# All 37 steps of the sample selection placed in the prompt attention, none in the first sample attention

## What is computed

```python
kx_past = pool_idx[page_table, layer].reshape(n, past, IDX_DIM)
_, idx = lax.top_k(indexer_scores(qx, concatenate([kx_past, kx], axis=1), wx, q_pos), ksel)
...
return gathered_softmax(q, kg, vg, q_pos[None, :, None] - idx, bias_tab)
```

## Time and profile before

| what | us |
|---|---|
| median of 3 runs (lowest, highest) | 3109.66 (3102.31, 3110.35) |
| the profiled execution's own time | 3110.44 |
| its span, first to last instruction | 3108.7 |
| PE busy, share of the span | 2667.9 (86%) |
| DVE busy, share of the span | 1139.3 (37%) |
| ACT busy, share of the span | 667.5 (21%) |
| POOL busy, share of the span | 373.4 (12%) |

### The profile page before, as it was taken

One profiled execution on the slowest core, in us unless ns is written; L12 is line 12 of the kernel. 1 busy time (PEld: TensorE's weight loads), 2 busy tenths in 40 slices (PEclk: granted clock), 3 DMA queues, 4 the chain that ended last, 5 costly groups with the idle time before them and its releaser, 6 DMA issues. The chain is left out here.

```text
span 3108.7 us, 34294 instructions
## 1 busy us (share of the span) xinstructions
PE 2667.9 (86%) x13764; PEld 1720.2 (55%) x13764; DVE 1139.3 (37%) x2070; ACT 667.5 (21%) x1356; POOL 373.4 (12%) x362
## 2 busy tenths in 40 slices
PE   6989989284788897886648669999999999999998
PEld 4444444142577776454325334566666666888843
DVE  0677889512466764584615113100000000000133
ACT  3222220032344543674303200100000000000011
POOL 1000000102434431000026510000000000000000
PEclk9999999686799998898769879999999999999999
DMA  6100101331345443405769762310110112110010
GB/s 249 47 35 35 43 30 43 127 84 58 95 125 159 127 127 105 135 29 169 252 203 377 287 231 102 115 41 27 40 40 27 40 40 95 38 38 30 11 34 33
DMA packets 169652, 304.83 MB, mean 98 GB/s; under 512 B 48536, under 2 KB 120408, under 8 KB 167226
## 3 DMA queue, kind: packets, MB, share of 16 engines
q1 hardware_dynamic: 143714, 172.54, 17.7%
q0 software_dynamic: 23936, 95.29, 8.4%
q10 hardware_dynamic: 1864, 35.08, 3.3%
HBM read 262.23 MB, written 67.77 MB: 106 GB/s over the span
## 5 line engine op out<-in xcount | busy, mean ns | idle before, releaser
L1020 PE MATMUL m_B<-m_big,m_wdB 128*128 128x363 f32 (+1 forms) x2112 | 646.1, 468 | 3.2 <-issue 3.2
L1020 PEld LDWEIGHTS m_B<-m_big,m_wdB 128*128 128x128 f32 x2112 | 400.5, 190 | 247.9 <-issue 4.8
L458 PE MATMUL i_psM<-i_w,i_xnT 128*128 128x462 f32 (+2 forms) x1152 | 424.7, 527 | 2.6 <-ACT i_xnT L288 2.3
L458 PEld LDWEIGHTS i_psM<-i_w,i_xnT 128*128 128x128 f32 x1152 | 219.0, 193 | 199.0 <-issue 179.0
L882 DVE TENSOR_TENSOR m_actT<-m_wdB,m_B 128x363 f32 (+3 forms) x66 | 35.2, 533 | 604.1 <-PE m_B L1020 604.1
L421 DVE MAX8 i_top<-i_work 128x8 f32<-128x384 f32 (+5 forms) x186 | 166.4, 894 | 6.3
L422 DVE MATCH_REPLACE8 i_work<-i_top,i_work 128x384 f32<-128x384 f32 (+5 forms) x186 | 162.8, 875 | 0.0
L774 ACT ACTIVATE m_wdB<-m_B 128x363 f32<-128x363 f32 (+1 forms) x66 | 31.2, 473 | 598.9 <-PE m_B L1020 598.9
L1062 PE MATMUL m_B<-m_wdA,m_actT 128*128 128x256 f32 x704 | 152.4, 379 | 0.8 <-DVE m_actT L882 0.8
L1062 PE MATMUL m_B<-m_wdB,m_actT 128*128 128x256 f32 x704 | 152.6, 379 | 0.0
L740 POOL TENSOR_TENSOR m_rstd<-m_ms,m_half 128x1 f32<-128x1 f32 x18 | 9.9, 551 | 1133.0 <-DVE m_ms L850 1133.0
(11 more groups left out here) (413 smaller groups left out, 3532.5 us busy)
## 6 DMA issues: line engine op xcount, KB each, us to landing
b_Kp<-b_k SPq DMA_DIRECT2D x32, 512.0 KB, 11.4
b_Vp<-b_v SPq DMA_DIRECT2D x32, 512.0 KB, 10.9
o_bk<-b_k ACTq DMA_DIRECT2D x8, 2040.0 KB
o_bv<-b_v ACTq DMA_DIRECT2D x8, 2040.0 KB
m_wdB<-w_gate SPq DMA_DIRECT2D x22, 512.0 KB, 3.9
m_wdB<-w_up SPq DMA_DIRECT2D x22, 512.0 KB, 5.2
i_w<-w_in POOLq DMA_DIRECT2D x5, 1848.0 KB, 35.5
proj<-i_stage SPq DMA_DIRECT2D x40, 231.0 KB, 2.0
```

What stands on the lines that cost most here:

```text
L458: mm = nc.tensor.matmul(psM[:, q % 2, 0:cols.stop - cols.start], xnT[:, t % RING, k, :], w[:, k, cols], start=(k == 0), stop=(k == KO - 1))
L1020: mm = nc.tensor.matmul(B[:, bank, 0:r1 - r0], wgu[:, i, u, k, :], hnT[:, k, r0:r1], start=(k == 0), stop=(k == KO - 1))
```

## The change

`S_EARLY` becomes `S_STEPS`: all 37 steps are spread over the 32 pairs of the prompt attention by the same weights. The first sample attention does no steps; its DVE begins with the memset that releases POOL's stores of the mask. Nothing else is changed, and no operation is added or dropped.

```diff
-S_EARLY = 22
+S_EARLY = S_STEPS
...
                     dve.wait_ge(S["own"], own_n[0])
 
-                steps = iter(range(S_EARLY, S_STEPS))
-
-                def select(count):
-                    for _, k in zip(range(count), steps):
-                        kth.step(own, k)
-                        if k == S_STEPS - 1:
-                            nc.vector.memset(kth.count[:, :], 0.0).then_inc(s_steps, 1)
-
                 def evac_keys(k, i):
...
                     nc.vector.tensor_copy(spreadb[:, :, :], spread[:, :, :]).then_inc(spread_at, 1)
+                else:
+                    nc.vector.memset(kth.count[:, :], 0.0).then_inc(s_steps, 1)
                 dve.wait_ge(turned, 1)
...
-                    if not sparse:
-                        select(2)
```

## The result

The changed kernel takes 3123.66 us (median of 5 runs, 3122.43 to 3129.28), the kernel before 3106.38 (5 runs, 3100.86 to 3110.35): the ratio over the runs is 1.0060, interval 1.0043 to 1.0077. By the medians it is slower by 17.3 us; the forecast was slower by 18.6, which made 3129 us on top of a profiled execution of 3110.4. The profiled execution took 3123.41 us, span 3121.6, 13.0 us more than the one of before.

The account below looks back on a forecast made before the run. No engine alone bounds the prompt: DVE fills pairs with steps, PE sets the others; DVE delays only the sample stage's end. 28.5 - 1.0 - 8.9 = +18.6 us on 3110.4 gave 3129, range 3117 to 3143.

Parts of the forecast that it names:

- Pairs 0 to 30: Prompt loop turns before the final one: added steps cost +28.5 us, 16.0 of 44.5 us fitting into DVE's waits.
- busy time divided by 0.947: Prompt stretches with steps in nearly every pair: DVE fills them, so they last its busy time divided by 0.947.
- Tail: Behind the prompt's final logits: -1.0 us, at most 1.7, as PE and ACT arrive with less backlog.
- the cover that I named: Prompt's tail: 1.7 us of PE and ACT work hides the longer steps ahead of the last reciprocal.
- Sample stage: First sample attention: without its steps the last softmax starts 8.9 us earlier, ends 6.8 and 10.5.
- "nothing" for the stores: Sample stage's front: POOL's mask stores among the first key loads cost nothing, up to +3.9 us without cover.
- the fixed chain: Sample stage behind the last softmax: value products and loads of values hang on it and move along unchanged.
- Step 0's wait: Prompt: step 0 moves from pair 5 to pair 3 with its wait for the scores, which costs nothing.
- Rival 1: Prompt: steps fill every DVE wait, costing only +18.1 us; total 3119, or 3117 with further ends; chance 0.13.
- Rival 2: Prompt tiles 5 to 7: PE idles and its clock falls to 1.2 GHz, priced at +10 us, 3139; chance 0.18.
- the fall at 1421.8: Kernel before, prompt's end: clock drops to 1.2 GHz after PE was busy 1.40 of 3.50 us, taken as support.
- Rival 3: Sample stage: its 15 steps held up all of it, so removal gives back 49.6 us, 3088; chance 0.04.

Follow-up runs that it names:

- e6: Against the kernel before: 17 steps in pairs 0 to 30, at most one each, 4 in the final pair, 16 at the sample stage's front; 3096.25 us, ratio 0.9958.
- e10: e6 with the release of the mask's stores moved behind the logits of chunk 5; 3092.44 us, ratio 0.9945 to the kernel before.
- e9: Against the kernel before: no steps in pairs 0 to 30, 4 in the final pair, 33 in the first sample attention; 3133.21 us, pairs 0 to 30 146.28.
- e3: The changed kernel with the memset that releases the mask's stores moved behind the last chunk's logits; 3127.94 us in one run, sample stage 132.03.
- e8: The changed kernel with the memset that releases the mask's stores moved behind the logits of chunk 5; 3122.04 us, ratio 1.0041 to the kernel before.
- e7: The changed kernel with its 37 steps spread evenly, one in every pair, two in pairs 9, 20 and 30, three in the final; 3126.56 us, pairs 0 to 30 173.83.
- e2: The kernel before without the 15 steps of its first sample attention, the mask set to zeros instead; 3099.08 us, ratio 0.9972, sample stage 130.71.

## Why the prediction was right

**Pairs 0 to 30: right, 1.7 us too high.** Forecast +28.5, measured +26.76. For tile 4 the changed kernel took 24.95 against a forecast of 24.8, for tile 5 29.07 against 29.3, tile 6 33.51 against 33.6, tile 7 26.08 against 26.2. The rule "busy time divided by 0.947" is what these tiles show (27.55 / 29.07 = 0.948; 31.77 / 33.51 = 0.948; tiles 4 and 7 show 0.935 and 0.954). The overshoot is in the early tiles: +1.2 instead of +2.0 in tiles 0-1 and 36.82 instead of 37.5 us in tiles 2-3. PE may work off more of its lag there than I allowed; no run shows it. Of 44.5 us added, 17.7 found room; I had said 16.0.

**Tail: right in sign, the reason half wrong.** Forecast -1.0 by less backlog, at most 1.7; measured -1.67. By the rows the final pair's first value products start 0.88 us sooner after the logits (1444.13 - 1436.95 = 7.18, before 1421.65 - 1413.59 = 8.06): that fits the smaller backlog that I named. They take 1.97 us instead of 3.62, as the clock is high here (mean 1.00 from 1436.95 to 1454.25) and was low before (0.90 over its final pair): -1.65, which I had not counted, although show the fall in front of them. Against that the reciprocal comes late by 1.39 - 0.53 = 0.86: the cover that I named was used up by that much. -0.88 - 1.65 + 0.86 = -1.67. e6 and e10 (low clock, tail 19.5) and e9 (high, 17.9), all three with four bit steps in the final pair and an early reciprocal, agree with that part. So the size of the tail is partly luck. Why the clock falls there in some kernels only is open: PE's last two gaps ahead of these products are 1.11 and 1.29 us in the kernel before and in the changed one alike.

**Sample stage: the size right (-8.9 against -8.8), two of its steps wrong.** The removed steps gave what was said: from the end of the products to the softmax 1.60 us instead of 10.48, -8.88. But "nothing" for the stores failed, and so did the fixed chain in which the value products were to move along. The stores stood among the first loads of keys, ACT's first move came at 22.35 us after the stage's start instead of 21.69, and the keys ended 2.75 us later (87.63 against 84.88); ACT's own issues were no cover, as the later loads of keys were waited for as well (17.5 us against 14.8). And from the softmax to the next stage it took 42.25 us instead of 44.91, -2.66. e3 and e8 show that these belong together: the kernel before pays for the stores too, among its values, and e8, which has them out of the way, takes 42.38 us (1588.03 - 1545.65). -8.88 + 2.75 - 2.66 = -8.79. The size came out right by luck: two errors made up for each other.

The Trainium skill, page "DMA: Bandwidth & Descriptors", section "Rules for kernel authors", says that spreading DMAs over the issuing engines gains no bandwidth, as all run on the same 16 DMA engines and interleave. The runs agree: POOL's 0.53 MB of stores lengthened the stage among SP's loads at either place, and the gap was worth 4.1 and 4.6 us in e8 (against the changed kernel and e3) and 3.3 in e10 (against e6).

**Step 0's wait:** its cost of nothing stands; DVE waits for nothing but products and its own `k_cut` (0.4 us) in these pairs.

**Rival 1** (floor +18.1) would have needed every wait of DVE. 13.8 us of them are still there, and e7 shows that even an even spread doesn't reach the floor. Its further end is 3116.3 us (3110.4 + 18.1 - 1.7 - 10.5), not 3117, which changes nothing.

**Rival 2** (the clock) happened in part, and cost nothing that the rows show. In pairs 0 to 30 the granted clock fell to its low level, 1.2 GHz, six times for a short while, once in each stretch from tiles 2-3 to tile 6 and twice in tile 7; ahead of each fall PE had waited 1.8 to 3.6 us for DVE (2.92 in tile 6). PE's waits for DVE in the prompt, before and after (us, times, longest):

```profile
PE p_psS L2509 <- DVE p_mx L2472: 5.6, 7, 1.5
```

```profile
PE p_psS L2509 <- DVE p_mx L2472: 22.6, 14, 3.6
```

By the means of 0.92, 0.95 and 0.87 the clock was low for a tenth to a quarter of tiles 5 to 7, where the rival's price took half. Busy time by stretch of tile 6's four pairs in the changed kernel (pairs 24, 25 and 27 have two steps, pair 26 one):

```profile
1377.36:1386.61 9.25, 7.99 (x82) 5.84 (x80) 8.76 (x21) 6.20 (x15) 0.00 (x0) 1.00 0.05 18
1386.61:1395.80 9.19, 6.46 (x33) 3.28 (x35) 8.70 (x21) 4.34 (x12) 0.00 (x0) 0.81 0.03 9
1395.80:1401.68 5.88, 5.55 (x48) 3.33 (x45) 5.60 (x15) 3.31 (x8) 0.00 (x0) 1.00 0.22 56
1401.68:1410.87 9.19, 8.31 (x89) 6.01 (x86) 8.70 (x21) 6.38 (x16) 0.00 (x0) 1.00 0.04 14
```

Pair 25, with a mean clock of 0.81, is as long as pair 27 at 1.00, and pair 24 as long as the 9.25 us of the earlier trace rows. DVE fills all three, and pair 25's products for keys still came after PE had waited 2.92 us for DVE. That is the room that the prediction set against this rival, though in tiles 5 to 7 it is about a quarter (24.55 busy in 33.6 leaves 27%) and not a third. The Trainium skill, page "TensorE: Matmul & The Clock Gate", section "Why this matters for your kernels", warns against idle gaps of PE between bursts of matmuls, since they halve the clock. The six falls agree in so far as each came behind such a gap. The fall at 1421.8, which the prediction set beside it, is a weaker case, as the same gaps of 1.11 and 1.29 us brought no fall in the changed kernel. The time of rival 2 did not follow, since another engine was the bound.

**Rival 3** is out by e2: all steps together hold the stage up by 9.6 us, not by 49.6.

## What to carry to other kernels

Work that is moved into another engine's shadow is free only up to the time that this engine needs, pair by pair: the first 17 steps cost 0.4 us in all, the last 12 bit steps with two finish steps 26.8. So before moving, compare what room the target has in each turn with what the old place really pays (9.6 of an estimated 49.6 us here), and split the work by that. A store that nobody waits for belongs where the DMA engines idle, not at the front of a stage or at its end.

## What was not expected of the hardware

- Six falls of the granted clock (means by tile of 0.87 to 0.95) left no trace where DVE fills the pairs: pair 25 took 9.19 us at 0.81 and pair 27 9.19 at 1.00. One fall in the tail, where PE is waited for, costs 1.65 us on one group of 32 matmuls (3.62 in the kernel before against 1.97).
- Three stores of 0.53 MB in 192 packets cost about 4 us among loads of values (47.5 to 48.2 against 42.5 to 44.0) and 3 to 8 us among the first loads of keys (87.63, 90.66 and 90.43 against 82.6 to 84.9), with much spread between executions. Of what they cost among the keys a part comes back behind them: at 90.7 and 90.4 us the rest is 42.6 and 42.5, at 87.6 it is 43.9.
